# Two edits to TensorE's queue in a four-layer kernel: 64-row products put side by side, and weight blocks of 512 features cut in two

## The reference

```python
# attention layer 0: part of it is differential attention, 4 heads, each with two 64-wide halves
p = masked_softmax(einsum('bthcd,bshcd->bhcts', qb, k) * dq ** -0.5, causal)
a = p[:, :, 0] - lam * p[:, :, 1]
...
# attention layer 1: an indexer of 16 heads, 64 wide, picks the keys
rel = relu(einsum('bthd,bsd->bths', qi, k_idx))
score = einsum('bths,bth->bts', rel, wi)
...
# recurrent layers: h = rms_norm(x), one wide projection h @ w_in (7952 columns), then four groups
# of 8 heads, 64 wide (retention, HGRN, mLSTM, RWKV), joined, projected, then gate/up/down
```

## Time and profile before

| | us |
|---|---|
| median of 3 runs | 3805.39 |
| lowest, highest of the 3 | 3795.68, 3811.14 |
| profiled execution, own time | 3798.66 |
| its span, first to last instruction | 3797.3 |
| TensorE busy in it | 3715.6 |
| mean granted TensorE clock | 0.990 of full speed |

### The profile page before, as it was taken

The page is one execution under the profiler, slowest core; times in us unless marked ns, Lnnn a source line. Parts: engine busy times, 40 slices in busy tenths (PEclk is TensorE's granted clock), DMA queues, the critical chain, the costliest instruction groups (busy, mean ns, idle before and its releaser), DMA issues.

```text
span 3797.3 us, 49231 instructions
## 1 busy us (share of the span) xinstructions
PE 3715.6 (98%) x19952; PEld 3149.2 (83%) x19952; DVE 2252.6 (59%) x3533; ACT 1798.7 (47%) x2523; POOL 114.9 (3%) x61
## 2 busy tenths in 40 slices
PE   9999999999999999999999999999999999999998
PEld 7886779787898998778888888888997778888887
DVE  5666666676566656765544444676566764454444
ACT  6565545456455325554444444655235454444443
POOL 0000000000010000000000000020000000000000
PEclk9999999999999999999999999999999999999999
DMA  7655456563555225456666655554234556666654
GB/s 232 201 157 181 140 158 176 161 188 111 182 169 151 64 72 167 164 160 189 188 189 189 202 193 193 177 155 138 58 116 134 179 162 191 189 189 189 204 193 168
DMA packets 341428, 628.37 MB, mean 165 GB/s; under 512 B 21088, under 2 KB 63024, under 8 KB 340432
## 3 DMA queue, kind: packets, MB, share of 16 engines
q1 hardware_dynamic: 331920, 611.53, 53.2%
q10 hardware_dynamic: 9280, 13.69, 1.1%
HBM read 623.04 MB, written 2.10 MB: 165 GB/s over the span
## 4 chain that ended last, share of the span: by engine, by line
PE 94%; DVE 3%; ACT 2%; DMA 1%; issue 1%; POOL 0%; ACTq 0%; SPq 0%; DVEq 0%; POOLq 0%
PE bank L647 80%; PE bank L775 1%; PE bank L1355 1%; PE bank L1452 1%; PE bank L2598 1%; PE bank L2612 1%; PE bank L2611 1%; DVE weights_low L541 1%; PE bank L2172 1%; PE bank L1435 1%; PE bank L2556 0%; PE bank L1358 0%; ACT weights_high L528 0%; DMA weights<-in_w_in_dram 0%; PE bank L1334 0%
## 5 line engine op out<-in xcount | busy, mean ns | idle before, releaser
L541 DVE TENSOR_TENSOR weights_low<-weights,weights_high 128x1024 fp32r<-128x1024 f32 (+2 forms) x1176 | 1401.7, 1201 | 934.0 <-ACT weights_high L528 923.0
L528 ACT ACTIVATE weights_high<-weights 128x1024 fp32r<-128x1024 f32 (+2 forms) x1176 | 1205.1, 1029 | 1294.8 <-PE bank L647 1234.2
L647 PE MATMUL bank<-weights_high,x_high 128*128 128x512 f32 (+3 forms) x2816 | 1105.9, 393 | 10.3 <-DVE weights_low L541 4.3
L647 PE MATMUL bank<-weights_low,x_high 128*128 128x512 f32 (+3 forms) x2816 | 1080.5, 384 | 0.0
L647 PE MATMUL bank<-weights_high,x_low 128*128 128x512 f32 (+3 forms) x2816 | 1079.9, 383 | 0.0
L647 PEld LDWEIGHTS bank<-weights_high,x_high 128*128 128x128 f32 x2816 | 531.2, 189 | 118.1 <-issue 12.8
L647 PEld LDWEIGHTS bank<-weights_low,x_high 128*128 128x128 f32 x2816 | 530.5, 188 | 101.2
L647 PEld LDWEIGHTS bank<-weights_high,x_low 128*128 128x128 f32 x2816 | 531.8, 189 | 93.0
L647 PE MATMUL bank<-x_high,weights_high 128*128 128x256 f32 x960 | 281.8, 294 | 13.8 <-DVE arena L676 9.9
L647 PE MATMUL bank<-x_low,weights_high 128*128 128x256 f32 x960 | 274.4, 286 | 0.0
L647 PE MATMUL bank<-x_high,weights_low 128*128 128x256 f32 x960 | 274.3, 286 | 0.0
(11 more groups left out here) (384 smaller groups left out, 3497.9 us busy)
## 6 DMA issues: line engine op xcount, KB each, us to landing
weights<-in_w_in_dram SPq DMA_DIRECT2D x208, 512.0 KB, 3.7
weights<-in_w_ffn_gate_dram SPq DMA_DIRECT2D x176, 512.0 KB, 3.6
weights<-in_w_ffn_up_dram SPq DMA_DIRECT2D x176, 512.0 KB, 3.6
weights<-in_w_ffn_down_dram SPq DMA_DIRECT2D x176, 512.0 KB, 3.6
weights<-in_w_out_dram SPq DMA_DIRECT2D x128, 512.0 KB, 3.7
weights<-in_even_w_in_dram SPq DMA_DIRECT2D x88, 512.0 KB, 3.7
weights<-in_odd_w_in_dram SPq DMA_DIRECT2D x80, 512.0 KB, 3.6
weights<-in_mem_w_kv_dram SPq DMA_DIRECT2D x32, 512.0 KB, 3.8
```

The lines of the kernel that those rows point to most:

```text
L528: self.high_mark[g] = self.high_split.count(act.ran(nc.scalar.activation(high, raw, ACT.Copy)), act.clock)
L541: self.low_mark[g] = self.low_split.count(dve.ran(nc.vector.tensor_tensor(low, raw, high.bitcast(F32), ALU.subtract)), dve.clock)
L647: ins = pe.ran(nc.tensor.matmul(out, l, r, start=(u + c + x + y == 0), stop=(u == blk.n - 1 and c == UNIT - 1 and y == 1)))
```

## The change

Two edits.

**Blocks with features.** `features` takes banks 0 to 3 for 512 columns as before; a block of 256 columns now takes banks 0, 1 or 2, 3 in alternation with its neighbours, and its unit has `at_once` = 4 chunks of 128 rows by 256 columns, again 512 KB. `halved` writes a block of 512 columns as two such blocks. All blocks of 512 columns but `hgf` are halved: rwr, rwk, rwv, mlq, mlk and hgq, the last of which moves from banks 4 to 7 into 0 to 3. `rwl` keeps its width, and its 8 units of 256 KB become 4 of 512 KB. A row piece of a load is 1 KB in these blocks instead of 2 KB.

**64-row products.** In `diff`, the scores of two units (the halves c = 0 and c = 1 of the same rows) are issued together into banks 4 and 5, which both have to be free. In the indexer two products are issued together, of different halves and of different row tiles t (128 and 256 columns), and two of the three banks have to be free. In the two `rwkv` stages both banks are filled in one go: the 128-row products of both halves first, then the two 64-row ones of the two halves, for each x.

```diff
+    def halved(self, name, AT, W, col, evac, scale):
+        self.features(name + "a", AT, W, col, 2, evac, scale=scale)
+        self.features(name, AT, W, col + 2 * P, 2, lambda n, b, mark: evac(n + 2, b, mark), scale=scale)
...
+    def features(self, name, AT, W, col, chunks, evac, scale=None):
+        banks = (0, 1, 2, 3) if chunks == 4 else (0, 1) if self.pair == 0 else (2, 3)
+        self.pair = 0 if chunks == 4 else 1 - self.pair
+        at_once = UNIT * TILE // (chunks * P)
+        self.add(Block(name, "features", self.by_unit(W, 0, D, col, chunks * P, at_once), D // (at_once * P), chunks * P,
+                       banks, evac, AT, 0, None, scale, at_once=at_once))
...
+        def scores_of_two(i):
+            first = [staged[units[i]["group"]]]
+            both = [*self.bank_free[4], *self.bank_free[5]]
+            yield first + both
+            pe.wait_ge(*first, *both)
+            for u, s, b in ((units[i], st[i], 4), (units[i + 1], st[i + 1], 5)):
+                s["bank"], s["ps"] = b, self.ps[b][:, 0:u["keys"]]
+                s["scored"] = pe.did(pe.ran(nc.tensor.matmul(s["ps"], u["qT"], u["kT"], start=True, stop=True)))
...
-            for e in range(2):
-                for t in range(T):
...
+            for first in range(2):
+                pair = [((first + t) % 2, t, (4, 5, 7)[(len(relued) + t) % 3]) for t in range(T)]
+                both = [m for e, t, b in pair for m in self.bank_free[b]]
+                yield both
+                pe.wait_ge(*both)
...
+        self.features(n + "hgf", L.hT, W, 5 * GW, 4, self.features_out(lambda j: room(HG, 4 + j), L.pre), scale=L.pre)
+        self.halved(n + "hgq", L.hT, W, 4 * GW, self.features_out(lambda j: room(HG, j), L.pre), L.pre)
...
+                both = [*self.bank_free[4], *self.bank_free[5]]
+                yield both
+                pe.wait_ge(*both)
+                summed = {}
+                for x in range(2):
+                    c = 2 * j + x
+                    for e in range(2):
+                        ins = pe.ran(nc.tensor.matmul(place(x, e), M4[4 * t + 2 * x + e][:, S:S + P], value(c, e), start=True, stop=(t == 0)))
+                        if x > t:
+                            summed[e] = pe.did(ins)
+                    if t:
+                        for e in range(2):
+                            ins = pe.ran(nc.tensor.matmul(place(x, e), tile(kk, c, 1)[head(e), :], s1(c, e), start=False, stop=True))
...
+                for x in range(2):
+                    c = 2 * j + x
+                    for e in range(2):
+                        n = 4 * t + 2 * x + e
+                        pe.ran(nc.tensor.matmul(place(x, e), M4[n][:, S + P:2 * S], value(c, e), start=True, stop=False))
+                        ins = pe.ran(nc.tensor.matmul(place(x, e), M4[n][:, P:2 * P], U[n], start=False, stop=(t == 0)))
+                    if t:
+                        for e in range(2):
+                            ins = pe.ran(nc.tensor.matmul(place(x, e), tile(r, c, 1)[head(e), :], s1(c, e), start=False, stop=True))
```

## The result

The kernel before and the changed kernel, on one chip: medians 3806.86 and 3780.74 us (four runs each, 3795.68 to 3811.14 and 3777.68 to 3785.64), ratio 0.9948 with a 95% interval of 0.9934 to 0.9963. On another chip the same pair gave 0.9957 (0.9944 to 0.9970), 3799.14 and 3782.73 us (17 and 6 runs). So the change gains 16 to 20 us, 0.43 to 0.52%, about the bound of 0.5%. The forecast was 3776 us and a gain of 26.5 us: the time is near it, but, as the experiments show, two large errors nearly cancelled.

What follows compares the result with a forecast made beforehand. TensorE, busy 98% of the span, was taken to bound the kernel. Gains of 13.1 us from blocks with features and 13.4 from 64-row products, 26.5 together, took 3802.0 to 3776 us; the 8 in 10 range was 3759 to 3797.

Steps and rivals of the forecast that it cites:

- Part 1: Blocks with features: alternating bank pairs end TensorE's waits for banks and the half clock behind them, a gain of 13.1 us.
- The four terms: Blocks with features: bank waits 9.9 us, new boundaries minus 1.7, half clock 3.4, late low part in rwl 1.5.
- the new boundary at hgf: One boundary per layer, hgf to hgq's first half, into banks just filled; two cost 1.7 us together.
- Rival (a): Blocks with features: bank waits return as waits for low parts of weights, so they gain nothing; 3789 us, chance 0.22.
- Part 2: 64-row products in differential attention, rwkv and the indexer: a pair costs what one product costs, a gain of 13.4 us.
- Differential attention, forecast 5.4: Scores: eight runs of lone 64-row products go, 4.2 us, with 1.2 us of lengthened neighbours; 5.4 us together.
- Rwkv, forecast 8.0: Two rwkv places: 32 excursions into 64 rows, pairs make two into one, 16 x 0.50 = 8.0 us.
- Indexer, forecast 0: Indexer: 16 pairs with the stream between them cost about what its 7 runs did; bounds +0.3 and -4.8 us.
- Rival (d): 64-row products: the pairs don't run side by side, 5.2 us less gain; 3781 us, chance 0.05.
- Rival (b): Rwkv stage: shorter excursions also spare 17 us at half clock, 8.5 us more gain; 3767 us, chance 0.12.
- (c): Indexer: the pairs stand two and two, up to 4.8 us more gain; 3771 us, chance 0.07.
- Rival (e): Loads of blocks with features: 1 KB pieces make the kernel slower, about 3864 us, chance 0.04.

Runs made afterwards that it cites:

- e1: Changed kernel with all 64-row products put back as in the kernel before, so only the blocks with features are changed: 3800.50 us, ratio 1.0002 to the kernel before.
- e9: Kernel with all pairs and halves in layer 0 alone, but hgq of layer 1 in banks 0 to 3: 3781.53 us, ratio 0.9956 to the kernel before.
- e5: Changed kernel with halves in layer 0 alone, hgq of layer 1 back in banks 4 to 7: 3768.60 us, ratio 0.9920; once more 3771.59, 0.9931.
- e2: Changed kernel with the blocks with features put back, so only the 64-row products are paired: 3778.12 us, ratio 0.9939 to the kernel before.
- e11: Kernel with all pairs and halves in layer 0 alone, but the indexer's products in their old order: 3768.53 us, ratio 0.9926 to the kernel before.
- e10: Kernel before with rwkv's common wait for both banks and evacuations behind both, but its products in the old order: 3805.57 us, ratio 1.0018.
- e7: Kernel before with the pairs of differential attention and the indexer alone: 3794.07 us, ratio 0.9986.
- e6: Kernel before with the pairs of rwkv alone: 3783.48 us, ratio 0.9959.

## Why the prediction came near, and where it was wrong

**Part 1, forecast 13.1 us, measured 0 (e1: 1.0002, so within 4 us).** The four terms are visible in layer 0, where e1 gains 4.3 us: 2.5 of idle time, 0.8 of clock, 1.0 of work. The bank waits went, and the new boundary at hgf cost nothing where 1.7 us were counted. Two terms were too large. In layer 1 a low part was not ready: against the 4.73 us at mlq stand 2.20 us in the changed kernel and 1.55 in e1, three units later. The prediction asked what is late next for the first two units only, and took its times, such as 2606.09, from VectorE's queue of the kernel before. Its reading of why VectorE was late is in part wrong too. Of the two low parts that VectorE waits for between 2606.09 and 2611.32, the first hangs on a unit that lands late; the second (first row) waits for ScalarE, which is busy with its own side work for rwkv without a pause before it (timelines of VectorE and ScalarE in the kernel before):

```profile
2610.18 1.22 DVE L541 TENSOR_TENSOR weights_low<-weights,weights_high 128x1024 fp32r<-128x1024 f32 x1 [0.92 <-ACT weights_high L528]
2607.51 1.69 ACT L2368 ACTIVATE arena<-arena 128x256 f32<-128x256 f32 x4
2609.10 1.04 ACT L528 ACTIVATE weights_high<-weights 128x1024 fp32r<-128x1024 f32 x1
```

An empty bank changes nothing in this, and it is the same work that holds VectorE at 2594.04 in the changed kernel. The other term is the 3.4 us of half clock, which stand behind the wait of 2.20 us as well (not behind the 1.55 us in e1).

The step that failed outright is the one that was not taken: the text asked what is late next at the place of each wait, but not what the new order does to VectorE some hundred us later. It priced hgq's move out of banks 4 to 7 as one more boundary, 0.83 us a layer; in layer 1 this move brings the stream's head start of 29 us and, with the waits and the half clock of e9 against e5, costs 10 us. That the head start costs the time is shown by e5 and e9. Why the planner sets the stream ahead is open: its code looks at the stream's bank in deciding whether a side step goes first, but e9, with as much head start, waits 6.1 us for banks, so a bank that is always free can't be the whole reason.

**Rival (a)** gave part 1 nothing, and in size that is what happened. Its mechanism is not: waits on the low parts rose by 2 us in e1, and the loss is the wait for retention's gate with its half clock. Its sign (over 5 us on line 541 in the features stretch) is not met: line 555 costs 3.2 us there.

**Part 2, forecast 13.4 us, measured 22 (e2: 0.9939).** Differential attention, forecast 5.4: in the stretch that holds it (317.8 to 524.3 in the kernel before) the work fell from 200.9 to 195.5 us, 5.4. Rwkv, forecast 8.0: at full clock, the products of the two places take 35.2 us in the kernel before (14.2 and 21.0) and 28.3 in e2 (10.7 and 17.6), so 6.9, or 0.43 an excursion where 0.50 were counted; by the ledger it is 2.0 + 3.3 = 5.3. I can't place the 1.6 us between them; the ledger takes all work at half clock as twice as slow, which is not exact. Indexer, forecast 0: 16 runs, as the bound of SLACK suggested, and 0 measured in e11. Rival (d) falls with the rows on the pairs. The rest of the 22 us is clock.

**Rival (b), the clock comes back too**, had a chance of 0.12 and is what happened: 8.9 us in layer 0, and some 2 us elsewhere. The evidence against it was "two of the other three rounds pass at full clock with the same excursions". That was read as a sign that the excursions don't matter, but it is one execution of something that differs from one to the next; the spread of the three runs shown, 15.5 us, was the hint that it does.

**(a) and (b) were set up as alternatives, each with part of the chance, but they concern different parts and can both hold.** Both together give 3802 - 13.4 - 8.5 = 3780, and the medians are 3780.74 and 3782.73. The forecast 3776 was near since 13 us that did not come and 9 to 11 us that had not been counted nearly cancel; that is luck. The 3802.0 us that the gain was taken from were 2 to 3 us above the kernel before in the larger groups. And the lower end of the range, 3759, is 3 us too high by its own words: (b) with (c) from the lowest run shown, 3795.7 - 26.5 - 8.5 - 4.8, is 3756.

**Rival (e), the loads,** did not come. A stretch of the changed kernel in which all pieces have 1 KB (2124 packets, all under 2 KB) answers to the earlier trace rows:

```profile
2448.00:2460.00 12.00, 11.53 (x97) 11.33 (x96) 5.71 (x9) 6.84 (x8) 4.65 (x2) 1.00 0.63 176
```

0.63 at 176 GB/s against 0.65 at 187 is 1.03 times as much a byte. The page of the Trainium skill, "DMA: Bandwidth & Descriptors", Why small descriptors are slow (HBM only), led to an estimate of 1.045, and the trace is near it at full rate as well. The pairs also speak on the strict order in start and end that the Trainium skill gives in "TensorE: Matmul & The Clock Gate", Part 3, The mechanism. As the prediction worked it out, a lone pair of 128 columns would by that rule take three passes and the fixed part, 0.53 us. It takes 0.42 us, as two passes do, so the trace does not agree with that reading of the rule.

**The signs.** Busy time fell by 15.9 us, over the 12 that would have spoken against the forecast; but "another place loses the clock for over 10 us" was met: two stretches of 10.2 us in layer 1. By this sign the prediction called itself wrong, and it pointed at the error. "No half clock behind rwl and mlq" was not met either. The signs of part 2 all came: 8 runs of 4 instructions in differential attention, 16 in rwkv, 16 in the indexer.

## What to carry to other kernels

In a kernel whose order is computed, an edit that frees one engine also moves the order, so ask of every step for which the stream's head start matters whether the side work still ends in time, and try the edit per layer and piece by piece: here the kernel with the halves in layer 0 alone is 14 us faster than the one with both layers changed, and one bank number in layer 1 costs 10 us by itself. Split a change before trusting its sum, for two parts with opposite signs can land on the forecast. Rivals that concern different parts are not alternatives: give each its own chance and write down the time for both.

## What the runs showed of the hardware

- Lone 64-row products between 128-row ones go with half clock while TensorE is busy without a gap: 17.1, 17.1, 13.7 + 13.7 and 3.4 + 3.4 us in rwkv of layer 0 in the kernel before, e1, e10 and e7, and 17.1 us in layer 1 of e10; with the same products side by side, none at these places in e2, e5, e6 and the changed kernel. This is worth 9 to 11 us, more than the 6.9 us of the products themselves. With the pairs of rwkv the times of a kernel spread by 1.5 to 8.0 us (4 to 6 runs each), without them by 8.9 to 16.5 (11 to 21 runs each).
- Two 64-row products on the two halves of the rows take 0.42 us from start to next start with 128 columns and 0.37 us with 64; one alone takes 0.42 and 0.36.
- A wait of 2.20 us was followed by 3.4 us of half clock (1.2 GHz) just as one of 4.73 us was, so to halve that wait saved its idle time alone. Behind 1.55 us at the same place in e1 there was none; and the same two waits of 2.19 and 1.20 us were followed by 10.2 us of half clock in the changed kernel and by none in e1, so the length of a wait does not settle it.
